# Latent-attention decode with the queries appended to the key weights, pages running through sequence borders, values on two array halves and paired rope scores

## What is computed

```python
def page_part(phys):                                   # one page, all 8 sequences
    k_nope, v, kpe = mla_expand(cache[phys], w_kvb, g_kn)   # keys: latent @ w_kvb, then RMS-normed per head
    sc = mla_scores(q_nope, q_pe, k_nope, kpe)              # q_nope . k_nope + q_pe . kpe, scaled
    m = sc.max(axis=-1)
    e = jnp.exp(sc - m[..., None])
    return m, e.sum(axis=-1), jnp.einsum('nhsk,nkhd->nhsd', e, v)
```

## Time and profile before

| | us |
|---|---|
| time, median of 3 runs | 2290.98 (2285.2 to 2292.43) |
| the profiled execution, its own time | 2288.8 |
| its span | 2287.0 |
| PE busy | 2065.7 (90%) |
| DVE busy | 1140.2 (50%) |
| ACT busy | 806.5 (35%) |
| mean granted clock of PE | 0.942 |

### The profile page before, as it was taken

How to read it: one execution, slowest core, us unless ns; L and a number is a source line. 1 busy time by engine, 2 the same in 40 slices (tenths; PEclk the granted TensorE clock), 3 DMA queues, 4 the chain that set the end, 5 groups by cost and what they waited for, 6 DMA issues and landing times.

```text
span 2287.0 us, 34057 instructions
## 1 busy us (share of the span) xinstructions
PE 2065.7 (90%) x13538; PEld 1747.9 (76%) x13538; DVE 1140.2 (50%) x1918; ACT 806.5 (35%) x1468; POOL 31.5 (1%) x57
## 2 busy tenths in 40 slices
PE   4897999999988778999869999888899999889997
PEld 1784899989976556999749999635677777669997
DVE  1462654369644436544475534586444334346532
ACT  1321443235433224432225422334334333225422
POOL 0000000000010000000000000000000000000000
PEclk8898999999989999999979999977899999899999
DMA  6774665644434976656646656320056456425442
GB/s 245 258 255 166 216 208 202 222 166 130 153 102 126 286 236 229 206 200 220 216 137 217 219 203 213 126 96 0 24 183 217 142 164 223 155 76 164 148 148 79
DMA packets 229500, 398.67 MB, mean 174 GB/s; under 512 B 9289, under 2 KB 195568, under 8 KB 215794
## 3 DMA queue, kind: packets, MB, share of 16 engines
q1 hardware_dynamic: 224912, 332.69, 44.0%
q0 software_dynamic: 3296, 59.76, 7.9%
q10 hardware_dynamic: 1161, 4.34, 0.6%
HBM read 391.23 MB, written 59.76 MB: 197 GB/s over the span
## 4 chain that ended last, share of the span: by engine, by line
PE 82%; DVE 8%; DMA 4%; ACT 3%; issue 2%; ACTq 0%; SPq 0%; POOL 0%; DVEq 0%; POOLq 0%
PE bank L1117 37%; PE bank L1023 11%; PE bank L1594 8%; PE bank L1036 4%; PE bank L988 4%; PE bank L1092 3%; PE bank L1204 2%; DVE rstd L1813 2%; PE bank L1401 2%; PE bank L1603 1%; DMA work<-in_ada_w 1%; DMA values_old<-in_state_swa 1%; PE bank L1346 1%; PE bank L1605 1%; PE bank L1082 1%
## 5 line engine op out<-in xcount | busy, mean ns | idle before, releaser
L1680 DVE TENSOR_TENSOR ring_lo<-ring,ring_hi 128x1024 fp32r<-128x1024 f32 (+1 forms) x324 | 380.1, 1214 | 363.4 <-ACT ring_hi L681 363.3
L681 ACT ACTIVATE ring_hi<-ring 128x1024 fp32r<-128x1024 f32 (+1 forms) x324 | 323.1, 1046 | 333.5 <-PE bank L1117 279.6
L1117 PE MATMUL bank<-hidden_hi,ring_hi 128*128 128x320 f32 x1024 | 318.9, 311 | 0.0
L1117 PE MATMUL bank<-hidden_hi,ring_lo 128*128 128x320 f32 x1024 | 316.4, 309 | 0.0
L1117 PE MATMUL bank<-hidden_lo,ring_hi 128*128 128x320 f32 x1024 | 316.3, 309 | 0.0
L1117 PE MATMUL bank<-h_hi,ring_hi 128*128 128x320 f32 x896 | 279.6, 312 | 0.1
L1117 PE MATMUL bank<-h_lo,ring_hi 128*128 128x320 f32 x896 | 276.2, 308 | 0.0
L1117 PE MATMUL bank<-h_hi,ring_lo 128*128 128x320 f32 x896 | 275.9, 308 | 0.0
L1117 PEld LDWEIGHTS bank<-hidden_hi,ring_hi 128*128 128x128 f32 x1024 | 192.2, 188 | 20.1 <-issue 20.1
L988 PE MATMUL bank<-tab,work 128*128 128x128 f32 (+6 forms) x708 | 128.8, 308 | 73.9 <-DVE latents_lo L2145 17.5
L1117 PEld LDWEIGHTS bank<-hidden_lo,ring_hi 128*128 128x128 f32 x1024 | 192.3, 188 | 0.0
(11 more groups left out here) (263 smaller groups left out, 3382.4 us busy)
## 6 DMA issues: line engine op xcount, KB each, us to landing
ring<-in_mlp_w SPq DMA_DIRECT2D x128, 1024.0 KB, 5.5
work<-in_ada_w SPq DMA_DIRECT2D x88, 1024.0 KB, 7.4
ring<-in_swa_w_qkv SPq DMA_DIRECT2D x18, 1024.0 KB, 5.0
out_swa_s<-in_state_swa POOLq DMA_DIRECT2D x8, 2016.0 KB, 10.3
ring<-in_conv_w_in SPq DMA_DIRECT2D x12, 1024.0 KB, 6.2
work<-in_state_swa SPq DMA_DIRECT2D x48, 256.0 KB, 9.1
work<-in_cache_mla SPq DMA_DIRECT2D x64, 160.0 KB, 2.2
ring<-in_ada_w SPq DMA_DIRECT2D x8, 1024.0 KB, 11.9
```

Of the source, the lines that this page charges most:

```text
L681: act.activation(ring_hi[:, place, part], ring[:, s, part], ACT.Copy).then_inc(sem("weights_hi"), 1)
L1117: mm = pe.matmul(bank[a % 4][:, 0:T], w[:, k, :], x(k), start=first and k == 0 and j == 0, stop=last and k == KD - 1 and j == 2)
L1680: dve.tensor_tensor(ring_lo[:, s, part], ring[:, s, part], ring_hi[:, place, part], ALU.subtract)\
```

## The change

All edits lie in the decode of the latent attention and in what prepares it.

- **Queries appended to the key weights.** The absorbed queries of the sequence stand behind the key columns of the last two heads in a buffer `md_tail`, one for each parity of the sequence, with high and low parts. A page's products are then 18 of 384, 384 and 320 columns (two halves of the latent, three pairings, three banks), where the last holds 256 key columns and 64 score columns. Banks 0 to 5 hold two pages. ACT copies the scores out to `md_raw`.
- **Paired rope scores.** The rope keys of two pages are turned into the two partition halves of one block (one 64-column turn and one fp32 product with the identity into partitions 64 to 127), and one fp32 product of 128 rows and 128 columns gives the rope scores of both; `md_qr` holds the rope queries on a block diagonal.
- **Pages running through borders.** PE, ACT and DVE no longer loop over sequences: one list runs over all 64 pages, written out. The turn of page k+1 stands ahead of the products of page k for every k. ACT squares page k-1 while page k is multiplied; the root, the exponential and the other steps of sequence n-1 are put at fixed pages of sequence n, those of PE in the middle of a page's products.
- **Values on two array halves.** Even pages accumulate in output partitions 0 to 63, odd ones in 64 to 127. A column of ones ahead of each page row (`PG = 1 + LAT`) makes the sum of weights column 0 of the same 257-column product. A product with `md_same` adds the two halves' sums; the turn of the result adds the two halves' values.
- **Preparation.** The key weights are split in four parts instead of two (2560 columns instead of 2048), the rope queries are also moved to partitions 64 to 127 by one fp32 product of 512 columns, and there are some more small clears and copies on DVE.
- SP waits for the first and the last four pages by semaphores of their own. Semaphores of the norms are shared between phases, and three of POOL's clears share one; the order on each engine stays.

```diff
-                        for i in range(2):
-                            for c in range(2):
-                                for y, z in pairings:
-                                    mm = pe.matmul(bank[2 * (x % 2) + i][:, :], lT_parts[y][:, c, x, :],
-                                                   kvb_parts[z][:, c, 512 * i:512 * (i + 1)],
...
+            def page_turn(n, j):
+                k, half = PAGES * n + j, n % 2
...
+                if k:
+                    pe.wait_ge(sem("md_latents_split"), k)
...
+                for c in range(2):
+                    mm = turn(bank[6][:, c * P:(c + 1) * P], md_pg[half][:, j, 1 + c * P:1 + (c + 1) * P], P)
+                if j % 2 == 0:
+                    turn(bank[6][0:ROPE, 2 * P:3 * P], md_pg[half][:, j, 1 + LORA:PG], P)
+                    mm = pe.matmul(bank[6][ROPE:P, 2 * P:3 * P], md_pg[half][:, j + 1, 1 + LORA:PG], ident, start=True, stop=True)
+                mm.then_inc(sem("md_turned"), 1)
...
+            def page_products(n, j, middle):
+                k = PAGES * n + j
+                pe.wait_ge(sem("md_latents_split"), k + 1)
...
+                if k >= 2:
+                    pe.wait_ge(sem("md_squared"), k)
+                banks = bank[3 * (k % 2):3 * (k % 2) + 3]
+                for c in range(2):
+                    for y, z in pairings:
+                        keys = kvb_parts[z][:, c, :]
+                        for dst, w in zip(banks, (keys[:, 0:384], keys[:, 384:AB], md_tail[n % 2][z][:, c, :])):
+                            mm = pe.matmul(dst[:, 0:w.shape[-1]], lT_parts[y][:, c, j, :], w, start=c == y == z == 0, stop=c == y == 1)
+                    if c == 0 and middle:
+                        middle(n - 1)
+                if j == PAGES - 1:
+                    mm.then_inc(sem("md_scored"), 1)
+                if j % 2:
+                    mm = pe.matmul(banks[2][:, TAIL:TAIL + P], md_rT[:, j // 2, :], md_qr[:, n, :, :].rearrange("p a x -> p (a x)"),
+                                   start=True, stop=True)
...
+            def page_values(n):
+                pe.wait_ge(sem("md_exp"), n + 1)
...
+                for b in range(PAGES):
+                    r = 64 * (b % 2)
+                    mm = pe.matmul(bank[7][r:r + 64, 0:1 + LORA], md_P[:, b, :], md_pg[n % 2][:, b, 0:1 + LORA],
+                                   start=b < 2, stop=b >= PAGES - 2)
+                    if b == 1:
+                        pe.matmul(own[:, AT_VALUES], new, ml_tok[0:TS, 2, 0:LORA], start=False, stop=False)
+                        pe.matmul(own[:, 0:1], new, ones[0:TS, 0:1], start=False, stop=False)
...
+            page_turn(0, 0)
+            for k in range(NS * PAGES):
+                n, j = divmod(k, PAGES)
+                if k + 1 < NS * PAGES:
+                    page_turn(*divmod(k + 1, PAGES))
+                page_products(n, j, {3: page_spread, 4: page_values, 5: page_total, 6: page_result}.get(j) if n else None)
+                if n and j == 2:
+                    page_max(n - 1)
+            for step in (page_max, page_spread, page_values, page_total, page_result):
+                step(NS - 1)
```

More of the change, by code:

```diff
@@ L290, in build @@
         both = taken[0]
+        assert both - 2880 >= PAGES * PG + 4 * PAST and 8 * TAIL <= 2880
         ml_V, ml_k, ml_s = area(2, H, VD), area(H, TP), area(3, TP)
@@ new lines, in page_max, with page_spread @@
+            def page_max(n):
+                pe.wait_ge(sem("md_max"), n + 1)
+                if n:
+                    pe.wait_ge(sem("md_out"), n)
+                turn(bank[7][:, AT_TURNED], md_m[:, 0:2, :].rearrange("p a x -> p (a x)"), P).then_inc(sem("md_max_turned"), 1)
+            def page_spread(n):
+                pe.wait_ge(sem("md_diag"), n + 1)
+                pe.matmul(bank[7][:, AT_SPREAD], ones[0:64, :], md_m[0:64, 2, :], start=True, stop=True).then_inc(sem("md_max_spread"), 1)
@@ new lines, in page_total, with page_result @@
+            def page_total(n):
+                pe.wait_ge(sem("md_sums"), n + 1)
+                pe.matmul(bank[7][:, AT_TOTAL], md_same, md_sum[:, 0:1], start=True, stop=True).then_inc(sem("md_total"), 1)
+            def page_result(n):
+                pe.wait_ge(sem("md_normed"), n + 1)
+                for c in range(2):
+                    mm = pe.matmul(bank[7][:, 320 + 64 * c:384 + 64 * c], md_tok[:, c * P:(c + 1) * P], md_same[:, 0:64], start=True, stop=True)
+                mm.then_inc(sem("md_result_turned"), 1)
@@ L2187, in _ @@
-            mla_pages(0, [lambda: None] * 4, lambda: None)
-            with dve.Fori(0, NS - 1) as n:
-                own.enter(n, 7)
-                mla_pages(n + 1, mla_steps(n), lambda: mla_masked(n))
-                own.leave(NS - 1)
-            mla_masked(NS - 1)
-            for step in mla_steps(NS - 1):
-                step()
+            page_lo(0, 0)
+            for k in range(NS * PAGES):
+                n, j = divmod(k, PAGES)
+                ahead = {3: page_max, 5: page_sums, 6: page_normed, 7: page_pick}
+                behind = {1: page_scaled, 2: page_added, 3: page_subtract}
+                if n and j in ahead:
+                    ahead[j](n - 1)
+                if k + 1 < NS * PAGES:
+                    page_lo(*divmod(k + 1, PAGES))
+                if n and j in behind:
+                    behind[j](n - 1)
+                if j == 3 and 2 <= n + 1 < NS:
+                    queries_lo(n + 1)
+                if k:
+                    page_reduce(*divmod(k - 1, PAGES))
```

411 lines of the change are left out of this document (196 added, 215 removed).

## The result

The changed kernel takes 2221.19 us (median of four runs, 2217.59 to 2224.36) against 2291.46 for the kernel before, 70.3 less: ratio 0.970, 95% interval 0.968 to 0.972. Forecast was 2213 with a range of 2196 to 2240. The profiled execution of the changed kernel is the slowest of its four: 2224.36 us (span 2222.5, mean granted clock 0.944), 64.4 less than the 2288.8 of the one before, where the sum had said 75.8.

What follows compares the result with a forecast made beforehand. PE was taken as the bound (busy 42.04 of 44.40 us a sequence). Pages -36.5, values -19.2, border -25.3, small steps +4.2, ahead of the stage +3.5, tail -2.5 sum to -75.8: from 2288.8 to 2213 us, range 2196 to 2240.

Steps and rivals of the forecast that it cites:

- A page: Page products, rope and turns on PE: 4.18 us falls to 3.61, over 64 pages -36.5 us.
- Values: Values of a sequence on two array halves running beside each other: 2.66 us against 5.40, -19.2 for seven.
- the rival of halves in turn: Values: products into the two halves do not overlap, +1.84 us a sequence, total 2227; chance 0.10.
- The border and small steps: Sequence borders: older products hide the root, -3.6 each, -25.3; broken products' pick-ups and the sum's product, +4.2.
- The stage's first sequence: Its eight pages, counted within the 64-page saving of -36.5 us, with full clock taken throughout the stage.
- The tail: Behind the last sequence: values and sums -3.7, sum's copy, product and waits give back 1.2, together -2.5 us.
- the chain stays: Behind the last sequence: same chain of waits as before, with PE idle and slow.
- the price of a pass: Values behind the last sequence: 18 passes in 6.32 us, 0.35 each, so ten in their place take 3.7.
- Between the own tokens' keys and the first turn: Stage start: rope-query product +1.5 us ahead of the keys, PE idle +1.4 (between 0 and 3) behind them.
- Ahead of these: DVE's split of key weights, 2048 to 2560 columns, ahead of the prompt attention's first scores: +0.6 us.
- late pages: Rival: page loads landing as late as POOL's window copy make six sequences wait, 94 us, total 2316; chance 0.03.
- The rows' start off 256 bytes: Page loads: rows starting 4 bytes off need six transactions for five, estimated 2.6 us for 2.2, hidden by slack.

Runs made afterwards that it cites:

- the run with the halves in turn: Changed kernel with all values of the even pages put ahead of those of the odd pages, no longer alternating; median 2228.5 us.
- the values later: Changed kernel with values, sum and result of a finished sequence one page later (pages 5, 6, 7 of the next instead of 4, 5, 6); median 2233.1 us.
- border with root: Changed kernel with the next sequence's first turn behind the last page's products, and last squares and root ahead of that page's copy; median 2260.9 us.
- full rows: Changed kernel with full-width rope turn, new stage-start order, and three 64-row products a sequence run over 128 rows, the upper 64 zeros; median 2194.5 us.

## Why the prediction was right

The direction and the size to within 8 us held, and so did the mechanisms of page, values and border. What failed lies at the two ends of the stage, where full gains and an unchanged chain were counted. All six misses listed below point the same way, so the closeness does not come from errors that cancel. The steps:

- **A page** was to fall to 3.61 and fell to 3.65. The 384-column products cost 0.175 to 0.177, as interpolated between 320 and 512. The turns were mis-sized: 0.92 for two pages, not 0.80, since the identity product costs 0.54, not 0.3. On the 56 pages of seven sequences that is 2.2 us.
- **Values** 2.66 forecast, 2.67 measured; the rival of halves in turn is refuted by its own run.
- **The border and small steps** were to leave 2.6 of a period and leave 34.40 - 8 x 3.65 - 2.67 = 2.53, in which the small steps were not measured one by one.
- **The stage's first sequence** was counted with full gains on all eight pages, -4.6. It gained 2.6: between the stage's first turn and the sequence's last rope score 37.11 before, 34.55 after. The first page gained nothing, since it waits for its split and runs at the low clock in both; here the prediction's full clock throughout was wrong. The next sequence's first turn, 0.78 us at 1664.99, now also lies inside this stretch.
- **The tail** was to gain 2.5 and gained 0.4. Two steps failed. The first is "the chain stays": what stands ahead of the values is 1.3 longer. Timelines of PE and ACT, the kernel before and then the changed one:

```profile
1973.66 0.43 PE L1605 MATMUL bank<-work 64*128 64x64 f32 x2
1979.67 0.47 PE L988 MATMUL bank<-tab,work 128*128 128x128 f32 x1 [5.58 <-DVE work L2017]
...
1973.18 0.60 ACT L935 ACTIVATE work<-bank 128x512 f32<-128x512 f32 x1 [3.23 <-PE bank L1594]
```

```profile
1908.79 0.39 PE L1598 MATMUL bank<-work 128*128 128x128 f32 x2
1916.06 0.48 PE L1035 MATMUL bank<-tab,work 128*128 128x128 f32 x1 [6.88 <-DVE work L2200]
...
1909.21 0.49 ACT L964 ACTIVATE work<-bank 128x384 f32<-128x384 f32 x1 [1.95 <-PE bank L1598]
```

ACT used to square while PE still made the query products and the rope score, and began 0.48 ahead of the latter. Now keys and scores come out of the same products, and it begins 0.42 behind it. With two more copies on ACT, of scores and rope scores, the idle before the maximum's turn grew by 1.3. The second is the price of a pass, 0.35, taken from 18 passes during which the clock rose (granted 0.50 up to 1986.0, then 0.81). The shorter values run at the low clock throughout. Windows as in the earlier trace rows, the values before and after:

```profile
1983.05:1989.30 6.25, 6.25 (x19) 3.24 (x19) 0.00 (x0) 0.00 (x0) 0.00 (x0) 0.66 0.90 283
...
1919.44:1924.50 5.06, 5.05 (x20) 2.27 (x20) 0.00 (x0) 0.00 (x0) 0.00 (x0) 0.50 0.65 207
```

They take 5.05 us where 3.7 was forecast, against 7.5 for values and sums before: 2.5 less, where the prediction has 3.7 (its own terms, 6.32 + 1.3 - 3.7, make 3.9). The sum's copy, product and waits give back 0.9 of the 1.2 counted.

- **Between the own tokens' keys and the first turn** the forecast of 1.5 + 1.4 stands against 1.9 for the rope product and 1.5 more idle (4.68 for 3.18), less 0.1 for shorter keys.
- **Ahead of these** the forecast was 0.6 (the split), and the changed execution is 4.6 later at the rope product. Of the same code up to there, the eleven profiles of the changed kernel and its variants start their own tokens' keys anywhere from 1614.0 to 1624.7:

```profile
L1552 PE MATMUL bank<-work x8: 592/1061/1114, 1623.8 to 1629.0; 128*64 128x512 f32 x8
```

```profile
L1552 PE MATMUL bank<-work x8: 592/1044/1114, 1614.0 to 1619.1; 128*64 128x512 f32 x8
```

(the changed kernel and the run with the halves in turn). In the pair of profiles the same instructions run 1.3 us later at 500 us, 11.4 at 849, and 6.8 at 1500; most of it comes in the sliding-window decode with its waits for state loads, where the change only joins three semaphores. The eleven start at 1620.8 in the mean, so some 3 of the 4 us are where this one execution lies among its like. Whether the last 1 is the change stays open, as there is one profile of the kernel before; where in that decode the scatter arises was not taken apart.

Together, against -75.8: pages +2.2, first sequence +2.0, tail +2.1, stage start +0.4, the code ahead +4.0 (some 3 of it scatter), behind the stage +0.7; that is -64.4.

Of the rivals, late pages were priced from a slack that is half as wide as I thought, or less. "About 10 us" from release to first turn was right (1758.62 to 1768.18 is 9.6). But the fourth page is issued 4.8 behind the release (1763.37 in SP's timeline) and lands at about 7, where I had 6 and took 4 as what is left. The rival was right that the loads would come to lie on the end of POOL's copy, and the stretched loads and issues above are what that costs; it stayed within the slack. The rows' start off 256 bytes does not show: the median is 2.2 in both kernels, and with the values later, free of the copy, the first four loads of five sequences land in 2.1 to 2.3. The Trainium skill, "DMA: Bandwidth & Descriptors", section How a descriptor splits into AXI transactions, lets a transaction start only at a 256-byte boundary, by which 1280 bytes that start off one take six for five. The prediction's estimate of 2.6 us from it is not what these loads show.

## What to carry to other kernels

Look for what is queued ahead of the copy that the next product needs, and give it a stretch of older products as cover: here undoing that alone cost more than undoing any one of the edits to the products (33 us against 9 to 26), and the cover has to outlast the whole queue (without cover PE idled 3.4 us a border with the root in the queue, 1.1 without). Count products by their changes of shape as well as by their columns: a small product of another shape cost 0.45 to 0.55 us for some 0.2 of passes, so pad it to the full shape, or let it ride in a wider one. When a loop gets shorter, recompute the slack of its loads, and look at what other queues do at that time: the slack fell to between 1.0 and 2.6 us here because the loads came to meet another engine's copy, and the next savings, 2.4 us a period, ran into it. And do not scale a price read from a stretch in which the clock changed: the tail's passes cost 0.35 in the mean of two clocks, and their shorter successors ran at the lower one alone.

## What the runs showed of the hardware that was not expected

- fp32 products of 64 output rows into alternating halves: twelve passes in 1.45 us, as long as six into one half (1.44).
- An idle of 1.1 us at each border left the granted clock at 1.00; of six idles of 1.3 to 1.7 us one was followed by the low clock; idles of 2.3 us (the kernel before) and of 3.4 us (border with root) were, seven times out of seven each.
- SP's issue of a 160 KB load takes 0.34 us, and in the kernel before all 64 do. In the changed kernel, where a sequence's loads start 1.9 to 3.5 us ahead of the landing of POOL's last transfer, the second issue takes 0.43 to 2.15 us; with full rows, where they start 2.8 to 4.9 us ahead, 1.35 to 3.30. That the meeting causes it rests on timing: the run with the values later moves the loads behind the landing, and its second issues take 0.34 to 0.45.
- The change to a product of 64 rows cost 0.09 more in the middle of the values than going on with 128 rows, half of them zeros (0.58 against 0.49).
